# Eight stage ends: the last copy out of PSUM is done behind the stage's end, and four runs of zero products are left out

## What is computed

```python
# first block, layer i
x = x + 0.5 * swiglu_ffn(x, ...)
h = rmsnorm(x, mix_norm[i])
x = x + (even_mixer if i % 2 == 0 else odd_mixer)(h, ...)   # projections, attentions, @ w_out
x = x + 0.5 * swiglu_ffn(x, ...)
# second block, layer i
z = rms_norm(h, norm_mix_g[i]) @ w_in[i]
o_a = rwkv7_branch(...); o_b = mla_branch(...); o_c = gdn_branch(...)
h = h + (g_a*(o_a @ w_br_rwkv[i]) + g_b*(o_b @ w_br_mla[i]) + g_c*(o_c @ w_br_gdn[i])) @ w_out[i]
h = h + (swiglu(u2, ...) if i % 2 == 0 else moe_swiglu(u2, ...))
```

## Time and the profile before

| | us |
|---|---|
| median of 3 runs (3115.74 to 3121.15) | 3116.46 |
| the profiled execution, its own time | 3118.85 |
| its span | 3116.8 |
| PE busy | 3057.5 (98%) |
| DVE busy | 1954.4 (63%) |
| ACT busy | 796.9 (26%) |

### The profile page before, as it was taken

The page is one execution under the profiler, slowest core; times in us unless marked ns, Lnnn a source line. Parts: engine busy times, 40 slices in busy tenths (PEclk is TensorE's granted clock), DMA queues, the critical chain, the costliest instruction groups (busy, mean ns, idle before and its releaser), DMA issues. The chain is left out here.

```text
span 3116.8 us, 47318 instructions
## 1 busy us (share of the span) xinstructions
PE 3057.5 (98%) x18746; PEld 1805.8 (58%) x18746; DVE 1954.4 (63%) x3355; ACT 796.9 (26%) x2086; POOL 156.0 (5%) x146
## 2 busy tenths in 40 slices
PE   9999999999999999999999999999999999999998
PEld 7858686784468577785685576864333333322223
DVE  7766786775477545633575546432577776677777
ACT  4514453351245243221352224231200000000000
POOL 0000000000000002300001104010100000000000
PEclk9999999999999999999999999999999999999999
DMA  7542145344424440133444421133799999999993
GB/s 291 185 183 116 55 162 216 126 185 158 168 89 175 176 183 28 68 116 137 171 175 176 173 81 67 56 142 132 300 408 415 419 418 418 363 418 419 419 418 135
DMA packets 81048, 665.42 MB, mean 213 GB/s; under 512 B 10528, under 2 KB 11168, under 8 KB 14144
## 3 DMA queue, kind: packets, MB, share of 16 engines
q1 hardware_dynamic: 78816, 655.41, 53.2%
q10 hardware_dynamic: 2016, 7.00, 0.6%
HBM read 661.33 MB, written 1.05 MB: 213 GB/s over the span
## 5 line engine op out<-in xcount | busy, mean ns | idle before, releaser
L4402 PE MATMUL psum<-ring,arena 128*32 128x512 f32 x5376 | 582.2, 592 | 0.0
L4402 PEld LDWEIGHTS psum<-ring,arena 128*32 128x32 f32 x5376 | 176.3, 110 | 399.6 <-issue 398.8
L886 PE MATMUL psum<-ring,arena 128*128 128x256 f32 x1760 | 397.8, 379 | 0.0
L886 PEld LDWEIGHTS psum<-ring,arena 128*128 128x128 f32 x1760 | 334.4, 190 | 45.5
L886 PE MATMUL psum<-ring,xT_norm 128*128 128x256 f32 x1320 | 305.3, 381 | 1.0 <-DMA ring<-in_ffn_w 1.0
L941 ACT ACTIVATE arena<-arena 32x128 f32<-32x128 f32 x880 | 269.6, 306 | 30.9 <-DVE arena L1075 21.2
L1000 DVE TENSOR_TENSOR ring<-ring 128x1024 f32<-128x1024 f32 x220 | 267.2, 1215 | 9.5 <-DMA ring<-in_ffn_w 3.1
L886 PEld LDWEIGHTS psum<-ring,xT_norm 128*128 128x128 f32 x1320 | 252.1, 191 | 35.9 <-DMA ring<-in_ffn_w 1.4
L4556 ACT ACTIVATE arena<-psum 128x256 f32<-128x256 f32 x84 | 32.5, 386 | 782.6 <-PE psum L4402 782.6
L906 PE MATMUL psum<-ring,arena 128*128 128x512 f32 x440 | 205.8, 592 | 0.0
L3253 PE MATMUL psum<-xT_norm,ring 128*128 128x256 f32 x832 | 184.1, 380 | 0.0
(11 more groups left out here) (647 smaller groups left out, 3923.4 us busy)
## 6 DMA issues: line engine op xcount, KB each, us to landing
ring<-in_moe_w SPq DMA_DIRECT2D x340, 1024.0 KB, 9.3
ring<-in_ffn_w SPq DMA_DIRECT2D x50, 2048.0 KB, 7.6
ring<-in_ffn_w SPq DMA_DIRECT2D x65, 1024.0 KB, 5.0
ring<-in_merge_w SPq DMA_DIRECT2D x16, 2048.0 KB, 8.3
ring<-in_feat_w SPq DMA_DIRECT2D x12, 2048.0 KB, 9.2
ring<-in_ev_in_w SPq DMA_DIRECT2D x4, 2048.0 KB, 9.1
ring<-in_od_in_w SPq DMA_DIRECT2D x4, 2048.0 KB, 9.6
ring<-in_merge_w SPq DMA_DIRECT2D x8, 1024.0 KB, 11.6
```

The costliest lines, as they stand in the source:

```text
L886: last = pe.matmul(psum[:, bank, 0:GROUP], a[:, k, :], w[:, k, :], start=(fresh and k == 0), stop=(k == KT // 2 - 1), skip_group_check=True)
L4402: last = pe.matmul(psum[part(j), r, :], xg[:, u.i, u.group // GROUPS, r * P + BLOCK * j:r * P + BLOCK * (j + 1)], m[:, j, :], start=(u.i = ...
```

## The change

At eight stage ends the last copy out of PSUM is no longer made before the end. The engine waits for the products in PSUM, the stage ends, and the copy is the first thing that an engine does in the next stage:

- even preparation: `fill(10)` by ACT; odd preparation: `fill(7)`, by DVE before, by ACT now;
- both attentions: the last group's copy to `oT` by DVE, now at the head of `mix_on_vector(dve, 0)` in the projection;
- both `prepare`: keys n = 6 (ACT) and n = 7 (DVE), now in `chains`;
- both `chains`: the sigmoid of gate 5 (ACT), now in `join_branches`.

The readers wait for the moved copies: `score(i)` of one group, P4 and S1 of the projection, the first `g_scores_of`, and in the joining stage `gate(2)` and `weigh(5)`. The banks of the gates in the joining stage are shifted by one, so that bank 5 is written last, and PE's second branch product now waits for all six sigmoids. The zero products behind the last work of both mixer preparations (7, 4) and both attentions (6, 6) are gone.

```diff
@@ SevenProducts.mix_on_vector
+        elif i == 0 and self.late_rows:
+            dst, bank, n = self.late_rows
+            dve.tensor_copy(dst, self.prog.psum[:, bank, 0:n * P].rearrange("p (k t) -> p k t", k=n)).then_inc(self.late_copied, 1)
+            dve.wait_ge(self.late_copied, 1)
         dve.tensor_tensor(self.a[out], self.a[a], self.a[b], op).then_inc(self.mixed, 1)
@@ SevenProducts.on_tensor
+        elif left[0] == "2" and self.late_rows:
+            pe.wait_ge(self.late_copied, 1)
@@ attention
             def score(i, g):
+                if i == late.group:
+                    pe.wait_ge(late_copied, 1)
...
-                        last = pe.transpose(psum[:, 7, i * S + b * P:i * S + (b + 1) * P], plain.source[:, b, i * P:(i + 1) * P], prog.ident)
+                        last = pe.transpose(psum[:, 6, i * S + b * P:i * S + (b + 1) * P], plain.source[:, b, i * P:(i + 1) * P], prog.ident)
...
-            stay_busy(prog, pe, 0, 6)
...
+                if i == total - 1:
+                    prog.late_rows, = g.out
+                    return
...
+            act.activation(late.dst, psum[:, late.bank, :], ACT.Copy, scale=-SCORE_SCALE).then_inc(late_copied, 1)
@@ even_mixer
-            stay_busy(prog, pe, 3, 7)
...
-            fill(10)
+            act.wait_ge(turned, 11)
...
-    attention(prog, groups, Arena(prog, turned_o.at), 4, {3: 4}, OutputTurn(o, oT[:, 0:2]))
+    attention(prog, groups, Arena(prog, turned_o.at), 4, {3: 4}, LateQueries(fill_to(10), fill_bank(10), 1), OutputTurn(o, oT[:, 0:2]))
@@ odd_mixer
-            pe.wait_ge(z_ready, 8)
-            stay_busy(prog, pe, 2, 4)
...
-            for f in (3, 5, 7):
+            for f in (3, 5):
                 fill(f)
+            dve.wait_ge(turned, 8)
...
-    attention(prog, groups, Arena(prog, turned_o.at), 11, {})
+    attention(prog, groups, Arena(prog, turned_o.at), 11, {}, LateQueries(fill_to(7), fill_bank(7), len(groups) // 2))
@@ chains
+                else:
+                    pe.wait_ge(keys_copied[0], 1)
+                    pe.wait_ge(keys_copied[1], 1)
...
+            act.activation(last_keys(0), psum[0:96, 6, :], ACT.Copy).then_inc(keys_copied[0], 1)
             for k in range(4):
                 exponentials(k)
...
-            squash(5)
+            act.wait_ge(gate_sum, 6)
...
+            dve.tensor_copy(last_keys(1), psum[0:96, 7, :]).then_inc(keys_copied[1], 1)
@@ prepare
-            for n, bank in ((0, 1), (2, 3), (4, 4), (6, 6)):
+            for n, bank in ((0, 1), (2, 3), (4, 4)):
...
+            act.wait_ge(heads_turned, 7)
...
-            for n, bank in ((1, 2), (3, 0), (5, 5), (7, 7)):
+            for n, bank in ((1, 2), (3, 0), (5, 5)):
...
+            dve.wait_ge(heads_turned, 8)
@@ join_branches
-    value_bank, gate_bank = psum[:, 4, :], lambda m: psum[:, 5 + m % 3, :]
+    value_bank, gate_bank = psum[:, 4, :], lambda m: psum[:, 5 + (m + 1) % 3, :]
...
+                elif m == 2:
+                    pe.wait_ge(early_squashed, 1)
...
-                    pe.wait_ge(squashed, 4)
+                    pe.wait_ge(squashed, 6)
...
+            act.activation(gates[5], psum[:, 5, :], ACT.Sigmoid).then_inc(early_squashed, 1)
             act.activation(squares[:, 1], by_head(g_y), ACT.Square).then_inc(head_squared, 1)
...
+                elif n == 5:
+                    dve.wait_ge(early_squashed, 1)
```

More of the change, by code:

```diff
@@ L315, in __init__ @@
         self.loads, self.queue = {}, nc.scalar
+        self.late_rows = None
         self.piece_loaded = [self.ctx.enter_context(nc.semaphore(f"piece_loaded_{i}")) for i in range(PIECE_SEMS)]
@@ L1185, in __init__ @@
         self.mixed, self.summed, self.made = (ph.semaphore(n) for n in ("rows_mixed", "weights_summed", "blocks_made"))
+        self.late_rows, prog.late_rows = prog.late_rows, None
+        if self.late_rows:
+            self.late_copied = ph.semaphore("late_rows_copied")
     def bank(self, name):
@@ L1442, in __init__ @@
         self.banks = {bank for bank, at in places}
+LateQueries = namedtuple("LateQueries", "dst bank group")
 class OutputTurn:
@@ L1449, in __init__, with attention @@
         self.source, self.dst = source, dst
-def attention(prog, groups, mem, ahead, between, plain=None):
+def attention(prog, groups, mem, ahead, between, late, plain=None):
     WIDE, AWAY, BEHIND = 2 * BANK, 2, 3
@@ L1474, in attention @@
         plain_turned, plain_copied = ph.semaphore("plain_turned"), ph.semaphore("plain_copied")
+        late_copied = ph.semaphore("late_queries_copied")
         @ph.block.tensor
@@ L1623, in exponentials @@
                 last.then_inc(probs, 1)
+            act.activation(late.dst, psum[:, late.bank, :], ACT.Copy, scale=-SCORE_SCALE).then_inc(late_copied, 1)
             if plain:
                 act.wait_ge(plain_turned, 1)
-                act.activation(plain.dst.rearrange("p i t -> p (i t)"), psum[:, 7, :], ACT.Copy).then_inc(plain_copied, 1)
+                act.activation(plain.dst.rearrange("p i t -> p (i t)"), psum[:, 6, :], ACT.Copy).then_inc(plain_copied, 1)
             for i in range(total + AWAY):
@@ L2444, in chains @@
         gate_sum, squashed = ph.semaphore("gate_sum"), ph.semaphore("squashed")
+        keys_copied = [ph.semaphore("last_keys_by_scalar"), ph.semaphore("last_keys_by_vector")]
+        last_keys = lambda n: kept.kT[0:96, 4 + 2 * n:6 + 2 * n, :].rearrange("p h t -> p (h t)")
         @ph.block.sync
@@ L3877, in join_branches @@
             "summed", "centred", "head_squared", "head_mean", "head_rooted", "inverted", "r_step", "g_step", "bonus_ready"))
-        gate_sum, squashed, branch_sum, weighted, joined = (ph.semaphore(n) for n in (
-            "gate_sum", "squashed", "branch_sum", "weighted", "joined"))
+        gate_sum, squashed, branch_sum, weighted, joined, early_squashed = (ph.semaphore(n) for n in (
+            "gate_sum", "squashed", "branch_sum", "weighted", "joined", "early_gate_squashed"))
         o_turned, merged_turned, bank_full = (ph.semaphore(n) for n in ("o_turned", "merged_turned", "bank_full"))
```

## The result

| | before | after |
|---|---|---|
| median, us (22 executions of each, same chip) | 3117.78 | 3121.11 |
| lowest to highest | 3115.74 to 3134.91 | 3118.02 to 3142.53 |
| ratio after / before, 95% interval | | 1.0032, [1.0020, 1.0044] |
| profiled execution, its own time | 3118.85 | 3140.84 |

The account below looks back on a forecast made before the run. PE hardly rests and bounds the kernel, so time leaves only at stage ends: 2.8 + 1.3 + 1.0 + 0.2 + 0.4 = 5.7 us off 3116.46 gives 3110.8; with 0.5 allowed for the clock, 3111.2, range 3107.5 to 3115.5.

Parts of the forecast that it names:

- If more than 6.4 us are missing: Closing sign of error: a shortfall above 6.4 us would mean a wait overlooked elsewhere, caused by the zeros or copies.
- Both attentions, 1.4 each: Attention ends: without six zero products the next stage opens 1.4 us earlier (342.86 less 341.45), twice, 2.8 us.
- The 0.5 behind the end: Behind both attentions: DVE's moved copy and its wait shift DVE's sums by 0.5 us, hidden by 1.1 us of slack.
- Both `prepare`, 0.65: Ends of `prepare`: the stage no longer waits for DVE's copy, 0.73 less some 0.1, so 0.65 us, twice, 1.3.
- Both `chains`, 0.5: Ends of `chains`: ACT's sigmoid of 0.60 us no longer holds the stage open, 0.5 us, twice, 1.0.
- Even preparation, 0.2: End of even preparation: 7 zero products and ACT's second fill go, DVE becomes last; 0.2 us, bounds 0.1 and 0.4.
- Odd preparation, 0.4: End of odd preparation: 4 zero products go, DVE's last fill moves, ACT becomes last; 0.4 us, bounds 0.3 and 0.6.
- the 0.5 allowed for the median: Behind the even preparation: a likely low-clock stretch costs at most 1.7 us; 0.5 us was allowed for it.
- The first rival: Openings are held by the next engine, or a copy behind an end is in the way: 3 us won, 3113.5; chance 0.17.
- The slower rival: Zeros kept the clock up: 1.7 us low stretch at each of four ends, 3117.6, or two each, 3124.4; chance 0.03.
- The other four: Openings held or copies in the way (0.17), more won (0.13), transfers take time back (0.02), transposes don't hold the clock (0.03).
- more is won: ACT and DVE arrive sooner at the preparations, even attention's low stretch falls away: 7.5 to 8 us, some 3109; chance 0.13.

## Why the prediction was wrong, point by point

- **"If more than 6.4 us are missing, I have overlooked a wait that the zeros or the copies caused elsewhere"** is what happened. The failed step is the first one of the sum: that a removed PE instruction is worth only what it takes at its own place, and that "what follows an opening moves with it". It moves in time, but against the packets of PE's instructions it moves by 40 to 42 places, and the prediction put that at nothing without having looked. The runs show the price: about 2.5 us of stop and half of 3.4 us of low clock in layer 0 (138.09 - 133.76 = 4.3 us above what the layer takes without a gap), about 1 us more stop in layer 1, and in 9 of 22 executions some 20 us more by low clock. For the 13 others this does not quite add up: -5.3 + 4.3 + 0.9 is -0.1, and they lie 2.4 us above before. Short low stretches (their mean clock is 0.996 to 0.998, that of before mostly 0.998) would fill most of it, but none of these executions was profiled, so where they lose it is not shown.
- **Both attentions, 1.4 each**: measured 1.20 and 1.23 (the even one from 50.25 to 49.05 in the run with 23 short products, which like the kernel before has one low stretch of 3.41 us there). Mis-sized by 0.2: P1 starts 0.60 and not 0.41 behind the last values. I had carried over the pause that stood behind the zeros. The 0.5 behind the end cost nothing, as priced: both projections last 26.26 us, before and after.
- **Both `prepare`, 0.65**: 0.51 and 0.52. **Both `chains`, 0.5**: 0.50 in layer 0 (134.26 to 133.76) and 0.49 to 0.51 in layer 1 once no gap is there on either side. **Even preparation, 0.2**: 0.19. **Odd preparation, 0.4**: 0.67, just above its bound of 0.6; with the zeros back and the copies moved it won 0.00, and with the zeros out and no copy moved 0.15, so it takes both.
- The terms measured come to 2.43 + 1.03 + 1.00 + 0.19 + 0.67 = 5.3 us against 5.7. With no stall on either side the medians differ by 5.5 (3117.12 and 3111.62). That this agrees so closely with 5.3 is partly luck: the intervals of the two ratios are 0.001 to 0.0015 to each side, 3 us and more, and the profile of the first has no low stretch behind the even preparation where that of the second has one, which costs 1.35.
- **The clock at the ends**: the low stretch behind the even preparation came as "likely", and its price is 1.35 (50.25 against 48.90 in the kernel before with the later request, whose profile has none). All nine profiles without the zeros have it (3.41 us in five, 6.83 in four), two of the three with them lack it; so the 0.5 allowed for the median was rather too small, by up to 0.9, and by 1.4 more where the stretch is 6.83 long (50.46 against 49.05 for the stage). No end got a new one: PEclk is 1.00 at the odd preparation, the odd attention and `prepare` of the changed kernel, below. By the rule of the Trainium skill's page "TensorE: Matmul & The Clock Gate", Part 4, the first and third of these, which end in transposes, should have shown it; the trace does not.

```profile
838.00:846.00 8.00, 7.39 (x59) 5.05 (x58) 3.76 (x4) 5.75 (x15) 0.00 (x0) 1.00 0.85 316
866.00:872.00 6.00, 5.41 (x43) 3.35 (x41) 3.64 (x4) 0.92 (x2) 0.00 (x0) 1.00 0.00 0
1243.00:1252.00 9.00, 8.39 (x69) 7.17 (x69) 6.42 (x11) 5.33 (x11) 0.00 (x0) 1.00 0.45 156
```

- **Sums.** Two of the prediction's sums do not come out. The first rival's 5.7 - 0.2 - 1.0 - 0.6 is 3.9 and not 3, which gives 3112.6 and not 3113.5; and by the bounds named at the ends the sum lies between 4.5 and 6.1, not 4.6 and 6.4. Neither comes near the measured time.
- **The rivals.** The slower rival named the right sign and the right object (zeros that kept the clock up), by the wrong mechanism: behind three of its four ends no low stretch came. Behind the even preparation it may be right in part (a low stretch in all nine profiles without zeros, in one of three with them), but that is 1.35 us and not the loss. It gave 3117.6 and 3124.4, and the changed kernel lies between, by chance. The other four didn't show: nothing was lost behind an end; of "more is won" only the odd preparation's 0.27 came, while the low stretch of the even attention stayed in every profile without zeros, and the mixture stage moved along (+0.49, within its scatter).
- **What the trace of before had shown.** The row `PE psum L2661 <- issue: 1.6` was in the trace of before, 1.57 us long and caused by nothing that the profile shows. I had looked at the stage ends alone. An unexplained stop of the engine that bounds the kernel was the sign that its position was owed to something that my change would shift.

## What to carry to other kernels

Look for PE's waits put down to "issue" in a kernel whose time PE sets, and hold them against the packets of the instruction queue: where a large transfer is asked for just ahead of a run of very short products, the position of the 256-instruction blocks decides whether PE runs dry. Adding or removing a few PE instructions anywhere earlier shifts that position, so a small edit should be measured with the count of instructions restored (a few short products at the start) before its own effect is believed. The cure tried here is to ask for the transfer a few microseconds later: 2.9 to 4.1 us later took away every gap and every long execution (0 of 31) with three counts of instructions, while 2.1 us was not enough with one of them. Whether one delay serves any count isn't shown; smaller pieces weren't tried.

## What the runs showed of the hardware

- Where PE ran dry, a packet of 256 of its instructions started 4.7 to 7.2 us behind the request of 4 MB of weights on the same 16 DMA engines, and PE stood still for 0.8 to 2.6 us, in products of 32 and 64 columns (once, for 1.01 us, ahead of one of 256). Where one started 0.13 or 0.89 us behind it, PE did not stop.
- PE ran dry 489 to 545 instructions behind the start of the last packet, so by this estimate it has about two blocks of 256 at hand (kernel after, 489 and 545; before, 513; weights 2.1 us later, 541; 95 products, 499).
- A stop of 2.2 to 2.5 us of PE in the dense part of layer 1, by a late packet or by a plain semaphore wait, went with 44 to 51 us at the lower clock in a third to over a half of the executions, with PE busy nearly all the while (47.79 of 47.79 us); once a stop of 1.01 us did. What followed in the other executions isn't profiled. In layer 0 stops of 2.56 and 2.13 us were followed by only 3.41 and 6.83 us.
- 44 float32 transposes in 5 us with a rest of 0.6 to 1.1 us behind them left the granted clock at 1.00.
- Two executions of one program can differ by 20 us in 3,120 on this ground alone; the median then tells less than the two heaps and their shares.
